# Mixer B of a hybrid decoder step: values and turned probabilities for two blocks of queries on the even steps, and one buffer for the attention outputs that the gates read

## The reference

```python
z = rms_norm(x, g_mix) @ w_in                  # 1032 x 2048 @ 2048 x 5632
qa, ka, va, ga, qb, kb, vb, gb = split(z)
oa = combine_patterns([dilated_prompt(qa, ka, va, d, w // d, slopes_a) for w, d in DILATIONS])
ob = banded_attention(qb, kb, vb, 1, 128, slopes_b, sinks)   # blocks of 128 queries
ya, yb = oa * silu(ga), ob * silu(gb)
h = x + concat([ya, yb]) @ w_out
y = h + (p @ w_ple) * sigmoid(rms_norm(h, g_ple) @ w_pg)     # then the final rms_norm
```

## Time and profile before

| | |
|---|---|
| median of 3 runs | 2354.61 us (2350.45 to 2357.32) |
| the profiled execution | 2353.89 us |
| its span, first to last instruction | 2352.1 us |
| busy in the span: PE, DVE, POOL, ACT | 2292.0, 902.2, 775.7, 573.8 us |
| granted TensorE clock, mean | 0.996 |
| mixer B, first scores to last values | 900.69 to 1350 us |

### The profile page before, as it was taken

How to read it: one execution, slowest core, us unless ns; L and a number is a source line. 1 busy time by engine, 2 the same in 40 slices (tenths; PEclk the granted TensorE clock), 3 DMA queues, 4 the chain that set the end, 5 groups by cost and what they waited for, 6 DMA issues and landing times.

```text
span 2352.1 us, 39273 instructions
## 1 busy us (share of the span) xinstructions
PE 2292.0 (97%) x15606; PEld 2180.9 (93%) x15606; DVE 902.2 (38%) x2322; ACT 573.8 (24%) x1574; POOL 775.7 (33%) x783
## 2 busy tenths in 40 slices
PE   4999999999999999999999999999999999999986
PEld 4999999999999999888888999999999999999986
DVE  7123333333333404444555534343232373222235
ACT  5122222222222212323544310220000030000374
POOL 2232222222222232211222233343333344555564
PEclk9999999999999999999999999999999999999998
DMA  5144444444453425445454454454343455444666
GB/s 195 60 128 93 102 120 98 104 119 97 102 118 94 105 76 150 130 142 146 141 156 142 126 167 143 151 149 104 92 103 87 120 166 136 111 116 108 190 193 233
DMA packets 533179, 300.62 MB, mean 128 GB/s; under 512 B 235156, under 2 KB 497316, under 8 KB 531708
## 3 DMA queue, kind: packets, MB, share of 16 engines
q1 hardware_dynamic: 455317, 255.73, 40.8%
q10 hardware_dynamic: 77680, 42.39, 6.3%
HBM read 231.67 MB, written 66.36 MB: 127 GB/s over the span
## 4 chain that ended last, share of the span: by engine, by line
PE 92%; DVE 4%; ACT 2%; DMA 1%; issue 1%; POOL 0%; DVEq 0%; SPq 0%; ACTq 0%; POOLq 0%
PE psum L1079 27%; PE psum L1081 26%; PE psum L1080 26%; PE psum L875 3%; PE psum L897 2%; PE psum L908 2%; PE psum L967 1%; PE psum L954 1%; PE psum L937 1%; DVE x_n L1570 1%; DVE act_lo L1561 1%; PE psum L984 1%; DMA x_in<-in_x_prompt 0%; POOL w_lo L831 0%; DMA w_raw_more<-in_w_ple 0%
## 5 line engine op out<-in xcount | busy, mean ns | idle before, releaser
L1079 PE MATMUL psum<-act_hi,w_hi 128*128 128x344 f32 x4032 | 1305.7, 324 | 7.6 <-POOL w_lo L831 6.1
L1081 PE MATMUL psum<-act_hi,w_lo 128*128 128x344 f32 x4032 | 1287.2, 319 | 0.0
L1080 PE MATMUL psum<-act_lo,w_hi 128*128 128x344 f32 x4032 | 1286.6, 319 | 0.0
L1079 PEld LDWEIGHTS psum<-act_hi,w_hi 128*128 128x128 f32 x4032 | 758.3, 188 | 19.8 <-issue 12.8
L1081 PEld LDWEIGHTS psum<-act_hi,w_lo 128*128 128x128 f32 x4032 | 757.8, 188 | 0.0
L1080 PEld LDWEIGHTS psum<-act_lo,w_hi 128*128 128x128 f32 x4032 | 757.6, 188 | 0.2
L829 POOL CAST w_hi<-w_raw 128x512 fp32r<-128x512 f32 (+1 forms) x352 | 225.3, 640 | 1474.0 <-PE psum L1081 1289.8
L831 POOL TENSOR_TENSOR w_lo<-w_raw,w_hi 128x512 fp32r<-128x512 f32 (+1 forms) x390 | 511.3, 1312 | 57.9 <-ACT w_hi L1504 29.6
L1673 DVE COPY prob_t<-psum 128x512 f32<-128x512 f32 (+1 forms) x56 | 35.5, 634 | 389.9 <-PE psum L908 389.9
L1958 DVE TENSOR_TENSOR t_gate<-psum,acc 128x344 f32<-128x344 f32 x48 | 24.7, 515 | 224.7 <-PE psum L1081 224.7
L1889 DVE TENSOR_TENSOR h_row<-psum,h_row 128x344 f32<-128x344 f32 x48 | 22.2, 513 | 213.5 <-PE psum L1081 213.5
(11 more groups left out here) (212 smaller groups left out, 1810.0 us busy)
## 6 DMA issues: line engine op xcount, KB each, us to landing
w_raw<-in_w_in SPq DMA_DIRECT2D x208, 256.0 KB, 3.1
w_raw<-in_w_pg SPq DMA_DIRECT2D x94, 256.0 KB, 2.8
w_raw<-in_w_out SPq DMA_DIRECT2D x64, 256.0 KB, 2.6
z_scratch<-stage ACTq DMA_DIRECT2D x72, 172.0 KB, 1.9
h_scratch<-h_row ACTq DMA_DIRECT2D x16, 516.0 KB, 2.7
x_in<-in_x_prompt SPq DMA_DIRECT2D x8, 1024.0 KB, 5.1
zq<-z_scratch SPq DMA_DIRECT2D x32, 256.0 KB, 3.8
out<-z_sq SPq DMA_DIRECT2D x128, 64.0 KB, 2.8
```

What stands on the lines that cost most here:

```text
L1079: pe.matmul(psum[:, bank, 0:T3], hi_w, hi_a[:, k, rows], start=(k == 0), stop=False, skip_group_check=True)
L1080: pe.matmul(psum[:, bank, 0:T3], hi_w, lo_a[:, k, rows], start=False, stop=False, skip_group_check=True)
L1081: return pe.matmul(psum[:, bank, 0:T3], lo_w, hi_a[:, k, rows], start=False, stop=stop, skip_group_check=True)
```

## The change

It does four things.

1. The values and the turning move to even steps and take two blocks at a time: at even `s` blocks `s - 4` and `s - 3` are multiplied with the values, and blocks `s - 2` and `s - 1` are turned (`TURN_B = 2`, `VALUES_B = 4`), both behind the scores of that step. `probt_b` holds two blocks, and the second block is turned into bank 7, which the values of the next key head also use; so TensorE waits there for `b_nat_copied` and `b_copied`.
2. ScalarE copies both banks after both are turned, with one increment of `b_copied` for two blocks; the first `NAT_B` copy moves from step 2 to step 1.
3. `o_in` is one buffer. Its load waits until the unit before has been gated, and lies 5 positions later.
4. Small tensors move to other addresses (`s_sc`, `s_row`).

```diff
-TURN_B = 3
+TURN_B, VALUES_B = 2, 4
+B_BANKS = (4, 7)
...
     for u in range(GATE0, ZPAIR):
-        put(16 * u, "o_load", u)
+        put(16 * u + 5, "o_load", u)
...
-                    if u < GATE0 + 2:
+                    if u == GATE0:
                         sp.wait_ge(sem("ak_stored"), STORED * 2 * PAIRS)
                         sp.wait_ge(sem("a_summed"), NCH * PAIRS)
                     else:
-                        sp.wait_ge(sem("y_gated"), u - GATE0 - 1)
+                        sp.wait_ge(sem("y_gated"), u - GATE0)
...
+                    first = s - VALUES_B
+                    if 0 <= first < QB and s % 2 == 0:
+                        if first % 4 == 0:
+                            pe.wait_ge(sem("o_copied"), 2 * (PAIRS + n) + first // 4)
+                            pe.wait_ge(sem("b_nat_copied"), 3 * (n // 2) + 1 + first // 4)
+                        pe.wait_ge(sem("b_copied"), QB // 2 * n + first // 2 + 1)
+                        for b in (first, first + 1):
...
+                    first = s - TURN_B
+                    if 0 <= first < QB and s % 2 == 0:
+                        if n or first:
+                            pe.wait_ge(sem("b_copied"), QB // 2 * n + first // 2)
+                        pe.wait_ge(sem("b_nat_copied"), nat_before(n_, s_))
+                        for b in (first, first + 1):
                             for h in range(2):
...
+                                pe.wait_ge(sem("b_scaled"), 16 * n + 2 * b + h + 1)
+                                for x in range(min(b + 1, 2)):
+                                    mm = pe.transpose(psum[:, B_BANKS[b % 2], 256 * h + x * P:256 * h + (x + 1) * P], prob_b[:, b % 4, h, x * P:(x + 1) * P], ident[:])
+                            mm.then_inc(sem("b_turned"), 1)
...
-                    if 0 <= b < QB:
-                        nk = BLK * min(b + 1, 2)
-                        act.wait_ge(sem("b_turned"), QB * n + b + 1)
+                    if 0 <= b < QB and s % 2 == 0:
+                        act.wait_ge(sem("b_turned"), QB * n + b + 2)
                         if n or b:
                             act.wait_ge(sem("b_summed"), QB * n + b)
...
+                        for blk in (b, b + 1):
+                            nk = BLK * min(blk + 1, 2)
+                            m = act.activation(probt_b[:, blk % 2, :, 0:nk], heads(psum[:, B_BANKS[blk % 2], :])[:, :, 0:nk], ACT.Copy)
+                        m.then_inc(sem("b_copied"), 1)
```

More of the change, by code:

```diff
@@ L92, with nat_before @@
 NAT_B = [("v", range(0, 4), 1), ("v", range(4, 8), 3), ("k", range(7, 8), 5)]
-TURN_B = 3
+TURN_B, VALUES_B = 2, 4
+B_BANKS = (4, 7)
+def nat_before(n, s):
+    return 3 * ((n + 1) // 2) + (sum(at_s < s for _, _, at_s in NAT_B) if n % 2 == 0 else 0)
 SETS = [(1920, 1, 128), (1536, 4, 96), (0, 16, 96)]
@@ L327, in build @@
         zkb, s_q = at(B0 + 4096, ("zkb", [P, S], F32), ("s_q", [P, S], F32))
-        knat_b, o_in0 = at(B0 + 18432, ("knat_b", [P, P], F32), ("o_in0", [P, T3], F32))
-        probt_b, o_in1 = at(B0 + 20480, ("probt_b", [P, 2, 256], F32), ("o_in1", [P, T3], F32))
-        o_in = [o_in0, o_in1]
+        knat_b, o_in = at(B0 + 18432, ("knat_b", [P, P], F32), ("o_in", [P, T3], F32))
+        probt_b, = at(B0 + 20480, ("probt_b", [P, 2, 2, 256], F32))
         bias_b, prob_b, s_ring, s_prod, s_prob, s_bias, s_prob_t = at(
@@ L334, in build @@
             ("s_prob_t", [P, 3, 32], F32))
-        s_sc, s_row = at(B0 + 23904, ("s_sc", [P, 3, HEADS], F32), ("s_row", [HEADS, 8], F32))
+        s_row, = at(B0 + 50592, ("s_row", [HEADS, 8], F32))
+        s_sc = small[:, 0:3 * HEADS].rearrange("p (t h) -> p t h", t=3)
         q_ring, kb, bprob_t, bnew_t = at(
@@ L941, in b_step @@
                 for n, s in walked(n_, s_, QB):
-                    b = s - TURN_B - 1
-                    if 0 <= b < QB:
-                        k0, nk = max(b - 1, 0) * BLK, BLK * min(b + 1, 2)
-                        if b % 4 == 0:
-                            pe.wait_ge(sem("o_copied"), 2 * (PAIRS + n) + b // 4)
-                        if b == 0:
-                            pe.wait_ge(sem("b_nat_copied"), 3 * (n // 2) + 1)
-                        if b == 4:
-                            pe.wait_ge(sem("b_nat_copied"), 3 * (n // 2) + 2)
-                        pe.wait_ge(sem("b_copied"), QB * n + b + 1)
-                        for x in range(nk // P):
-                            for h in range(2):
-                                mm = pe.matmul(psum[HD * h:HD * h + HD, 6, (b % 4) * P:(b % 4 + 1) * P],
-                                               v_nat[:, k0 // P + x, HD * h:HD * h + HD], probt_b[:, h, x * P:(x + 1) * P],
-                                               start=(b % 4 == 0 and x == 0), stop=(x == nk // P - 1), skip_group_check=True)
-                        mm.then_inc(sem("b_summed"), 1)
@@ L958, in b_step @@
-                for n, s in walked(n_, s_, QB):
-                    b = s - TURN_B
-                    if 0 <= b < QB:
-                        nk = BLK * min(b + 1, 2)
-                        if n or b:
-                            pe.wait_ge(sem("b_copied"), QB * n + b)
-                        for h in range(2):
-                            pe.wait_ge(sem("b_scaled"), 16 * n + 2 * b + h + 1)
-                            for x in range(nk // P):
-                                mm = pe.transpose(psum[:, 4, 256 * h + x * P:256 * h + (x + 1) * P], prob_b[:, b % 4, h, x * P:(x + 1) * P], ident[:])
-                        mm.then_inc(sem("b_turned"), 1)
+                    first = s - VALUES_B
@@ new lines, in b_step @@
+                    if 0 <= first < QB and s % 2 == 0:
[4 more added lines that the diff above has]
+                        for b in (first, first + 1):
+                            k0, nk = max(b - 1, 0) * BLK, BLK * min(b + 1, 2)
+                            for x in range(nk // P):
+                                for h in range(2):
+                                    mm = pe.matmul(psum[HD * h:HD * h + HD, 6, (b % 4) * P:(b % 4 + 1) * P],
+                                                   v_nat[:, k0 // P + x, HD * h:HD * h + HD], probt_b[:, b % 2, h, x * P:(x + 1) * P],
+                                                   start=(b % 4 == 0 and x == 0), stop=(x == nk // P - 1), skip_group_check=True)
+                            mm.then_inc(sem("b_summed"), 1)
@@ L974, in b_step @@
                             pe.wait_ge(sem("b_nat_copied"), 3 * g + gi)
+                        if n_ or s_ > TURN_B:
+                            pe.wait_ge(sem("b_copied"), QB // 2 * n_ + (s_ - 1) // 2)
                         for x, blk in enumerate(blks):
@@ L1341, in b_step @@
                     for gi, (what, blks, at_s) in enumerate(NAT_B):
-                        if at_s + (gi == 0) == s and n % 2 == 0:
+                        if at_s == s and n % 2 == 0:
                             act.wait_ge(sem("b_nat_turned"), 3 * g + gi + 1)
@@ L1803, in _ @@
                     dve.wait_ge(sem(f"o_loaded{u % 2}"), 16 * ((u - GATE0) // 2 + 1))
-                    dve.tensor_tensor(stage[:, u % 2, 0:w], stage[:, u % 2, 0:w], o_in[u % 2][:, 0:w], ALU.mult).then_inc(sem("y_gated"), 1)
+                    dve.tensor_tensor(stage[:, u % 2, 0:w], stage[:, u % 2, 0:w], o_in[:, 0:w], ALU.mult).then_inc(sem("y_gated"), 1)
                 elif e[0] == "a":
```

9 lines of the change are left out of this document (4 added, 5 removed).

## The result

| | before | changed |
|---|---|---|
| median of the runs | 2354.61 us | 2363.90 us (2362.48 to 2368.94, 5 runs) |
| ratio, with its 95% interval | | 1.0044 [1.0033, 1.0055] |
| the profiled execution | 2353.89 us | 2366.57 us |
| its span | 2352.1 us | 2364.8 us |
| granted TensorE clock, mean | 0.996 | 0.991 |

The changed kernel is 9.3 us slower, 0.4%, a little over the 0.3% that I had called the bound of "no change". The time lies inside the range for 8 in 10 (2346 to 2366), but outside the forecast's own range (2350 to 2362), nearest to rival B, and on the other side of the bound from the likeliest case.

The account below looks back on a forecast made before the run. It took TensorE, busy 2292.0 of 2352.1 us, to bound the kernel. 2353.9 - 8.3 - 1.5 + 10.6 + 2.0 = 2356.7, so a median of 2357 us; own range 2350 to 2362, 8 in 10 2346 to 2366.

Parts of the forecast that it names:

- rival B: Mixer B from 1105 us: late scales delay copies, gating, loads and the next even step; 20 to 24 us waits, 2366; chance 0.20.
- the likeliest case: Whole kernel: median within 0.3% of the kernel before, so no change that a measurement can tell; chance 0.62.
- Part 1, the gaps: TensorE in mixer B: 32 groups of values and turning fewer, 0.26 us saved per pair, 8.3 us in all.
- Part 2, the wait for turned values: TensorE in mixer B: the 1.5 us of waits for copied turned values go; new waits at bank 7 cost nothing.
- Part 3, scales asked for too soon: Even steps of mixer B: turning asks for VectorE's scales in the same step; 10.6 us of TensorE waits.
- Part 4, one buffer: Gates' input: late load delays a gating near 1178 us, 1.5 us wait, 0.5 for other places, 2 us together.
- A: Mixer B: gaps worth 12 to 14 us, VectorE keeps up, late steps cost 4 us; 2343 to 2345; chance 0.15.
- C: Mixer B: merging saves only 4 us as matmuls in a row drain all the same, waits remain; 2361; chance 0.15.
- A new row: TensorE's list of waits: turning waiting for the scales, 9 to 13 us in 6 to 9 times.
- The gaps from 28 to about 14: TensorE: idle time before weight loads of values and turning falls from 28 to about 14 us, groups half as many.
- The longest wait at the step near 1220: TensorE in mixer B: the longest wait of turning for scales, 3 to 5 us, at the step near 1220 us.
- the signs of being wrong: Scales' wait row under 4 or over 18 us; main matmul after 1350 us over 7 off; new wait after mixer B.

Follow-up runs that it names:

- the kernel with odd steps: Changed kernel with turning and values of two blocks on the odd steps (turning s - 3, values s - 5), scores alone on even steps: 2352.24 us, ratio 0.9992.
- the first: Changed kernel with turning and values two steps later (turning s - 4, values s - 6), single buffer kept: 2350.20 us, ratio 0.9983 to the kernel before.
- the sixth experiment: Changed kernel, turning and values two steps later, sample rows' steps 2, 3 and following load 6 positions later: 2347.39 us, ratio 0.9958; also called the fastest version.
- the last experiment: Changed kernel with VectorE taking the step (scales, bias) ahead of the gating where both share a position: 2358.79 us, ratio 1.0017 to the kernel before.
- the held kernel: Kernel before with TensorE made to wait for unneeded exponentials at step 6 of pairs 1 to 6: 2394.85 us, ratio 1.0166.

## Why the prediction was right and wrong

The sum had +2.8 us against the profiled execution; that of the changed kernel is +12.7. The signs of the terms were right, and the decisive one, the scales asked for too soon, was there. But that the time fell inside the range is owed to the room left for rival B and not to the sum: with the waits and gaps as they turned out, and without the clock, which stood in no term, the same sum gives 2353.9 - 9.9 - 1.5 + 15.9 = 2358.4.

- **Part 1, the gaps: right, 0.26 a pair against 0.31.** 32 such pairs would give 9.9 us instead of 8.3; not all of them saved it (the one at 1270 us saved nothing). Taking the price from the rows of starts was sound. The estimate from the Trainium skill, "TensorE: Matmul & The Clock Gate", section "Back-to-back issue gap", 3.8 us in all, was not: 0.31 us a pair is more than twice its 0.12.
- **Part 2, the wait for turned values: right.** The 1.5 us went, and bank 7 brought no wait. What the prediction says of it, that each copy would show if ScalarE's exponentials ran late, is what the kernel with odd steps did.
- **Part 3, scales asked for too soon: right in the mechanism and near in size, off in the places.** Without the step at 1178 I had 10.6 us; measured are 15.9 - 3.4 = 12.5 in ten waits. The five steps that I had named with 1.0, 2.1, 2.4, 3.7 + 1.1 - 1.2 and 0.8 have 0.6, 1.4, 2.2, 2.7 and 0.7, so the allowance for a nearer even step was too much (that GpSimd's last split would miss the scales at the fourth was right: they took 2.26 us there instead of 3.54). The one that I had put at 0.5 took 4.2, because VectorE met GpSimd's `w_lo` three times in a row. "I count the meetings that the trace has" was the weak step: where they fall shifts with every us, and the fullest stretch of VectorE should have been charged for it. Rival B had allowed for more such meetings. The Trainium skill, "SBUF — State Buffer", section "Who interferes with whom", has it as an exclusive lock, and the trace agrees: the product that takes 0.68 us alone took 1.78 beside a split of 1.44.
- **Part 4, one buffer: right in the place and the chain, mis-sized.** 1.5 us at the step at 1178; measured are 3.38. By then the stream is 2.7 us earlier than before, and in its times I had the load out at 1176.7 and landed at 1179.1 to 1180.5. It went out at 1177.2, behind two loads for the sample rows instead of one, and took 4.6 us to land. Rows 9 have a median of 3.8 and 9.4 at worst, and I had taken it from the lower half. With small loads at the old positions this wait was gone; with the scales ahead of the gating it was gone too.
- **Missed altogether: the clock behind a wait.** 7.5 us, the largest error, and the reason that the time is beyond the bound. Every term of mine priced a wait of TensorE by its length. The waits of the sum came out 3.3 us too small, the gaps 1.6 too small; with the 7.5 of the clock that is 2.8 + 3.3 - 1.6 + 7.5 = 12.0 of the 12.7. The fit is a little better than the account: mixer B alone lost 14.0, so 2.0 there have no name, and 1.1 came back at 1480 us, where the kernel before waits 2.45 us and the changed one 1.31.
- **Rivals.** A: the gaps were not worth more than 10 us, and VectorE did not keep up. C: the saving is there, as the streams of the first and the sixth experiment show. B gave 2366 with 20 to 24 us of waits, each dearer than the last; the waits were 15.9, and the clock made the rest. So its time was near and only half of its reason. That two of the late steps (1178, 1122) hang on the gating ahead of the scales is shown by the last experiment. That a late step makes the next one late, which is B's own chain, no run shows.
- **What would show it.** A new row of 9 to 13 us in 6 to 9 times: 15.9 in 11. The gaps from 28 to about 14: about 18. The longest wait at the step near 1220: it was at 1178. VectorE waiting for `o_in` at one to three gates: two within mixer B, 9.2 us together. Of the signs of being wrong one came: the first main matmul behind the last values was to be no more than 7 us off, and it is 13 to 14 late. By its own measure the prediction had the stretch wrong, though its time was in range.

Left open: what makes the clock fall behind one wait and not behind the next of the same length; the 2.0 us of mixer B without a name; and the later losses of the fastest version, 3.4 of its 9.0 us between 1346 and 2200 us, of which 1.4 go at 1915, where the wait of L1191 is 1.9 us and was 0.5. None was tried further.

## What to carry to other kernels

When a change joins steps of a chain across engines, set the end of the producer against the new time of asking, for every step, and charge the fullest stretch of the producer for the meetings that may come. Price a wait of TensorE inside a dense stream at its length and, from 3 us on, at about half as much again (here 4.3 us cost 6.5); for shorter ones that surcharge is a risk and not a rule. Such a loss is best met by giving the chain more time: the same merging that lost 9 us won 8 with turning two steps later and the sample rows' steps moved behind the late gating.

## What the runs showed of the hardware

- TensorE's clock fell to half for 3.4 or 6.8 us at short waits in the middle of a stream at full speed. Between 60 and 2320 us the eleven traces have fourteen waits of TensorE of 2.86 us or longer, the six of 4.2 to 4.5 in the held kernel among them, and each has half clock at its end or within 1.6 us behind it. Below that it went either way: 2.16 without and 2.21 with it at the same step of two kernels, 2.55 at 1223 us without and 2.42 at 1293 us with it in one, 2.84 without and 2.79 with it in two others. It went either way even for 1.31 us, at the same matmul (L1057) of two kernels: none in the changed kernel at 1491.98, and in the one with the sample rows' steps moved

```profile
1470.55 0.20 PE L1057 MATMUL psum<-ident,bprob 16*128 16x16 f32 x1 [1.31 <-DVE bprob L1806]
...
1471.40:1474.80 3.40, 3.40 (x12) 0.50 0.35 107
```

- So the length of one wait does not tell whether the clock falls. The levels read were 0.50 and 1.00; the page "TensorE: Matmul & The Clock Gate" of the Trainium skill, "Part 1: The HAM clock gate", names two states of the gate, 1.2 and 2.4 GHz, and the trace agrees.
- This stands in no row of waits. It is seen in the granted clock of a table of stretches, or in starts of equal matmuls 0.286 us apart instead of 0.157; the busy share of TensorE hides it, since a stretch at half clock counts as fully busy (3.40 of 3.40 us from 1184.0 on).
- The executions of one kernel differ by it too. Of the 29 of the kernel before beside the first four experiments, the ten with a mean granted clock of 0.995 have a median of 2353.0 us and the five with 0.992 one of 2357.8. So a profiled execution is one draw, and stretches of half clock in it need not be those of the median run.
